# Two half projections of layer 1 moved into the last stage of layer 0

## The chip, the cores and the metric

The kernel runs on one core of a Trainium2 chip. The metric is the device time of one execution in microseconds; several runs are taken, and their median counts. Engines run side by side and meet only at semaphores: TensorE (PE) multiplies, VectorE (DVE), ScalarE (ACT) and GpSimd (POOL) work elementwise, SyncE (SP) issues most of the DMAs.

## The reference

A trunk of two layers on 1024 tokens of width 1024, all in float32. Each layer is `x = x + rmsnorm(mix(rmsnorm(x)))` and then `x = x + rmsnorm(ffn(rmsnorm(x)))`. Layer 0 (even) mixes with two kinds of attention, layer 1 (odd) with a sliding window of 128 tokens, 16 query heads, 2 key/value heads and a learned sink for each head. What matters here is the seam between them:

```python
h = rmsnorm(x, g[0])                       # layer 1, x is layer 0's result
q, k, v = split_cols(h @ w_qkv, ODD_SIZES) # 1024 x 1024 by 1024 x 1280
q, k = partial_rope(q, cos, sin), partial_rope(k, cos, sin)
```

and before it layer 0's down projection, `(gelu(gate) * val) @ w_out`, with 2816 rows in `w_out`.

## The kernel before, in words

**Products in three passes.** Each float32 factor is held as a hi part (rounded to fp32r) and a lo part (the rest), and each product is hi*hi + hi*lo + lo*hi. `three_passes` (L121) issues that for one weight block of 128 x 128 and one or two halves of 512 columns; every matmul in it loads its weights. A weight tile of 128 columns has 8 blocks (KT = 8), so a tile over both token halves is 8 x 3 x 2 = 48 matmuls, over one half 24. The hi part of a weight tile is an ACT copy of the loaded tile (L1968 in the trunk, L862 in the odd front), the lo part a subtraction on GpSimd (L2055, L985) or on VectorE (L2238).

**The trunk stage.** `trunk_stage` (L1722) is run once for each layer. It does the output projection of the mixer, the two norms around it, the 44 up tiles (NT_UP) with convolution and gate, and 66 down tiles (NT_DOWN = 3 x 22). The down projection goes in three passes over the 22 tiles of `w_out`, for token blocks 0 to 3, then 4 and 5, then 6 and 7 (BLOCKS). A down tile of the last pass is 2 blocks x 2 halves x 3 = 12 matmuls into ps[2] and ps[3]. The weights go round a ring of three hi/lo slots (`down_slot`, L1828) and four raw buffers (`raw_down`).

**The end of layer 0.** When a block's down product is complete, the block is normalised: ScalarE squares and sums it (`first`, L1930), VectorE scales it and adds x (`mix`, L2178, `add`, L2195), ScalarE stores it and squares it again (`second`, L1942), VectorE makes h, the normalised input of layer 1 (`scale`, L2197, the operation at L2206). TensorE turns h with 8 transposes (`turn`, L2064), and ScalarE and VectorE split what was turned into `act.hi` and `act.lo` (L1955, L2213). For blocks 0 to 5 that lies between later down tiles. Blocks 6 and 7, the last two, are turned behind all down tiles (L2171), into ps[0] and ps[1]. GpSimd has nothing to do in the down tiles.

**Between the stages** all engines meet at the end of the block, the semaphores of the stage are cleared (`recycle`, L103) and there is a barrier.

**The start of layer 1.** `OddFront` (L701) is the part of layer 1's trunk stage up to the output of the mixer. It projects h with 10 weight tiles: the keys (N_KEY = 0), the values (N_V = 1), eight of queries (from N_Q = 2). `project(n)` (L1038) writes prod[n % 2], which is ps[0] or ps[1], hi weights first (L375) and the lo pass behind them (L381). `take(n)` (L864, L872) copies it out. The order on the engines is written out by hand:

- TensorE: project(0), project(1) with rot(KEY) (L1027) behind its third block, project(2) with `turn_values(0)` (L1030, L1035) behind its third block, project(3) with turn_values(1) and rot, and so on. rot needs take(0); turn_values needs take(1).
- ScalarE: hi(0), hi(1), take(0), hi(2), pack_keys (L878, needs the rope of the keys), take(1), hi(3), take(2), hi(4), ...
- VectorE: rope(KEY) (L1158, L1159, L1162), the keys' lo parts (L1169), the copies of the turned values, then the ropes of the queries.
- SyncE loads tile n when the lo part of tile n - 2 is made (L828).

act.hi[0] and act.lo[0] hold token half 0, which is blocks 0 to 3; act.hi[1] and act.lo[1] hold blocks 4 to 7.

Of the kernel before, what the change touches and what calls it, by code (L numbers as in the profile page):

```python
# [6 lines left out]
F32 = mybir.dt.float32  # L7
# [8 lines left out]
P = 128  # L16
T = 1024
# [60 lines left out]
class Stage:  # L78
# [4 lines left out]
    def __init__(self, nc, name):  # L83
        self.nc, self.name, self.ctx = nc, name, ExitStack()
# [616 lines left out]
class OddFront:  # L701
# [5 lines left out]
    NG = 4 * TB  # L707
    LAST_SLOT = 4 * TB + 4

    def __init__(self, nc, g, st, base, act, new_act, w, sinks, w_mix, mix_rows, x_src, x_mid, gains, ps, stats, x_in, x_out, gain_in,  # L710
                 sq1, iv1, sq2, iv2, mixed, summed, h_ready):
        self.nc, self.g, self.act, self.new_act = nc, g, act, new_act
        self.w, self.sinks, self.w_mix, self.mix_rows = w, sinks, w_mix, mix_rows
# [10 lines left out]
        self.mraw = [at(f"mraw{k}", [P, D], F32, K + 32 * KB + 4 * KB * k) for k in range(KT)]  # L724
        self.mlo = [at(f"mlo{k}", [P, D], F32R, K + 32 * KB + 4 * KB * k) for k in range(KT)]
        W = K + 64 * KB
        self.raw = [at(f"raw{i}", [P, KT, P], F32, W + 4 * KB * i) for i in range(2)]
        self.w_hi = [at(f"w_hi{i}", [P, KT, P], F32R, W + 4 * KB * (2 + i)) for i in range(2)]
        self.w_lo = [at(f"w_lo{i}", [P, KT, P], F32R, W + 4 * KB * (4 + i)) for i in range(2)]
        self.prob = [at(f"prob{i}", [P, self.PAIRS, P], F32, W + 2 * KB * i) for i in range(2)]  # L730
        self.pT = [at(f"probT{i}", [P, self.PAIRS, P], F32, W + 2 * KB * (2 + i)) for i in range(2)]
        self.o = at("o", [P, 2, 2 * self.PAIRS, HD], F32, W + 8 * KB)
# [94 lines left out]

    def sync(self, sp, load_up):  # L828
        wv = self.w.rearrange("(k p) c -> p k c", p=P)
        for n in range(self.N_ALL):  # L830
            if n >= 2:
                sp.wait_ge(self.lo_done, n - 1)
            sp.dma_start(self.raw[n % 2][:], wv[:, :, self.COLUMN[n]:self.COLUMN[n] + P]).then_inc(self.w_in[n % 2], 16)
            if n == 1:
                sp.dma_start(self.sink[:].rearrange("p i s -> p (i s)"), self.sinks.partition_broadcast(P)).then_inc(self.sink_in, 16)
        sp.wait_ge(self.prod_done, self.N_ALL)
        for k in range(KT):
            for i, r in enumerate(self.mix_rows(k)):
                sp.dma_start(self.mraw[k][HD * i:HD * i + HD, :], self.w_mix[r:r + HD, :]).then_inc(self.m_in[k], 16)
        sp.wait_ge(self.q_lo, 32)  # L840
        sp.dma_start(self.g1[:], self.gains[0].partition_broadcast(P)).then_inc(self.gain_in, 16)
        sp.dma_start(self.g2[:], self.gains[1].partition_broadcast(P)).then_inc(self.gain_in, 16)
        rows = self.x_src.rearrange("(b p) d -> b p d", p=P)
        for b in range(TB):
            if b == 0:
                sp.wait_ge(self.rope_done, len(self.ROPED))
            else:
                sp.wait_ge(self.x_out[(b - 1) % 2], 16 * ((b - 1) // 2 + 1))
                sp.wait_ge(self.h_ready, b)
            sp.dma_start(self.x[:], rows[b]).then_inc(self.x_in[b % 2], 16)  # L850
            if b == TB - 2:
                load_up(0)
                load_up(1)

    def scalar(self, sc, split_w):
        N_KEY, N_V, N_Q, N_ALL, NG = self.N_KEY, self.N_V, self.N_Q, self.N_ALL, self.NG

        def hi(n):
            sc.wait_ge(self.w_in[n % 2], 16 * (n // 2 + 1))
            if n >= 2:  # L860
                sc.wait_ge(self.prod_done, n - 1)
            sc.activation(self.w_hi[n % 2][:], self.raw[n % 2][:], ACT.Copy).then_inc(self.hi_done, 1)  # L862

        def take(n):  # L864
            sc.wait_ge(self.prod_done, n + 1)
# [21 lines left out]
        def exp(n):  # L887
            nk = self.keys_of(self.where(n)[1])
            sc.wait_ge(self.nb_ready, n + 1)
            if n == 0:  # L890
                sc.wait_ge(self.lo_done, N_ALL)
# [86 lines left out]
    def gpsimd(self, pool, up_lo):  # L978
        pool.memset(self.v_even[:, :, :, HD:VW], 1.0).then_inc(self.ones_set, 1)
        pool.memset(self.v_odd[:, :, :, HD:VW], 1.0).then_inc(self.ones_set, 1)  # L980
        for n in range(self.N_ALL):
            pool.wait_ge(self.hi_done, n + 1)
            if n >= 2:
                pool.wait_ge(self.prod_done, n - 1)
            pool.tensor_tensor(self.w_lo[n % 2][:], self.raw[n % 2][:], self.w_hi[n % 2][:].bitcast(F32), ALU.subtract).then_inc(self.lo_done, 1)  # L985
        for k in range(KT):
            pool.wait_ge(self.m_hi, k + 1)
            pool.tensor_tensor(self.mlo[k][:], self.mraw[k][:], self.mhi[k][:].bitcast(F32), ALU.subtract).then_inc(self.m_lo, 1)
        for b in range(TB):
# [24 lines left out]
    def tensor(self, pe):  # L1014
# [21 lines left out]
            mm.then_inc(self.v_turned, 1)  # L1036

        def project(n):  # L1038
            pe.wait_ge(self.hi_done, n + 1)
            if n >= 2:  # L1040
                pe.wait_ge(self.taken, n - 1)
            outs = [self.prod[n % 2][:, h] for h in H]
            for k in range(KT):
                hi_weight_passes(pe, outs, self.w_hi[n % 2][:, k, :], [x[:, k, :] for x in act.hi], [x[:, k, :] for x in act.lo], k == 0)
                if k == 2 and n == N_KEY + 1:
                    rot(N_KEY)
                if k == 2 and n == N_Q:
                    turn_values(0)
                if k == 2 and n == N_Q + 1:
                    turn_values(1)  # L1050
                if k == 2 and n > N_Q + 1:
                    rot(n - 1)
                if k == 5 and n == N_Q + 1:
                    rot(N_Q)
            pe.wait_ge(self.lo_done, n + 1)
            for k in range(KT):
                mm = lo_weight_pass(pe, outs, self.w_lo[n % 2][:, k, :], [x[:, k, :] for x in act.hi], k == KT - 1)
            mm.then_inc(self.prod_done, 1)

        def scores(n):  # L1060
# [658 lines left out]
    return act  # L1719


def trunk_stage(nc, g, name, layer, act, w_mix, mix_rows, w_in, w_out, gains, x_src, x_mid, x_dst, onward, odd_mixer=None):  # L1722

# [79 lines left out]

    with Stage(nc, name) as st:
        st.sb("arena", [P, (194 * KB + 512 if odd_mixer else 129 * KB) // 4])
        ps = [st.ps(f"ps{i}", [P, T]) for i in range(4)]
# [14 lines left out]
        odd = odd_mixer and OddFront(nc, g, st, base, odd_input, act, *odd_mixer, w_mix, mix_rows, x_src, x_mid, gains, ps,  # L1823
                                     ([ss1, ss2], [std1, std2], [inv1, inv2]), x_in, x_out, gain_in[0],
                                     sq1, iv1, sq2, iv2, mixed, summed, h_ready)

        pass_of = lambda d: d // FT
        down_slot = lambda d: (NT_UP + d) % 3  # L1828
# [19 lines left out]
        with nc.Block() as block:  # L1848
            @block.sync
            def _(sp):  # L1850
# [59 lines left out]
                for d in range(NT_DOWN):  # L1910
# [13 lines left out]
                    if d == 2 * FT + 8:  # L1924
                        load_x(TB + 6)
                        load_x(TB + 7)

            @block.scalar
            def _(sc):
# [108 lines left out]
                for e in range(4, FT):  # L2038
                    prepare(2 * FT + e)
                    if e in (7, 8):  # L2040
                        split_h(TB + e - 3, ps[e - 7])
                first(TB + 6, ps[2])
                first(TB + 7, ps[3])
                second(TB + 6)
                second(TB + 7)
                split_h(TB + 6, ps[0])
                split_h(TB + 7, ps[1])
                for i in range(2):
                    sc.wait_ge(x_out[i], 16 * TB)

# [1 line left out]
            def _(pool):  # L2052
# [5 lines left out]
                    odd.gpsimd(pool, lo)  # L2058
                for u in range(2 if odd else 0, NT_UP):
                    lo(u)  # L2060

            @block.tensor
            def _(pe):
# [95 lines left out]
                for d in range(NT_DOWN):  # L2159
# [6 lines left out]
                    if d in (2 * FT + 4, 2 * FT + 5):  # L2166
# [1 line left out]
                        if onward:  # L2168
                            pe.wait_ge(mixed, TB + n + 1)
                        turn(TB + n, ps[n - 4])  # L2170
                for n in range(6, TB):  # L2171
                    if onward:
                        pe.wait_ge(lo_done, TB + n - 1)
                    turn(TB + n, ps[n - 6])

            @block.vector
            def _(dve):
# [126 lines left out]
                for n in range(TB + 6, TB + 8):  # L2304
                    scale(n)
                for n in range(TB + 6, TB + 8):
                    split_h(n, ps[n - TB - 6])


def build(nc, x, positions, norm_gains, even_w_in, even_b_forget, even_w_out, odd_w_qkv, odd_sinks, odd_w_out,  # L2310
# [5 lines left out]
    with Stage(nc, "main") as st:  # L2316
# [55 lines left out]
        with Stage(nc, "rest") as rs:  # L2372
# [6 lines left out]
            trunk_stage(nc, g, "l0", 0, act, even_w_out[0], lambda k: [P * k], ffn_w_in, ffn_w_out, (row(0, 1), row(0, 2), row(0, 3), row(1, 0)),  # L2379
                        x[0], x_mid, x_odd, True)  # L2380
            Stage.recycle(nc)
        trunk_stage(nc, g, "l1", 1, act, odd_w_out[0], lambda k: [HD * (4 * (k // 2) + k % 2), HD * (4 * (k // 2) + 2 + k % 2)], ffn_w_in, ffn_w_out, (row(1, 1), row(1, 2), row(1, 3), None),
                        x_odd, x_mid, out[0], False, (odd_w_qkv[0], odd_sinks))


_INS = ['x', 'positions', 'norm_gains', 'even_w_in', 'even_b_forget', 'even_w_out', 'odd_w_qkv', 'odd_sinks',
# [14 lines left out]
```

## Time and profile before

| | |
|---|---|
| median of 3 runs | 2650.26 us (2639.95 to 2651.22) |
| the profiled execution | 2648.2 us |
| its span | 2646.4 us |
| TensorE busy | 2476.6 us |
| mean granted clock of TensorE | 0.97 |
| end of the last down tile of layer 0 | 1545.6 us |
| first DMA issue of layer 1's stage | 1559.91 us |
| first matmul of layer 1 | 1564.88 us |

The profile is of one execution. Times in its rows are microseconds from the span's start; the granted clock is in parts of TensorE's full speed, 1.00 for 2.4 GHz. Matmuls overlap each other: what counts is the distance from start to start. In the timeline "x8" means eight instructions in a run, and the time in brackets is the idle time of the engine before them, with what ended it.

### The profile page before, as it was taken

The numbers are of one execution on the slowest core, as the hardware profiler recorded it, in microseconds if no ns is written. First come the engines' busy times: TensorE is split into PE (matmuls) and PEld (weight loads), VectorE is DVE, ScalarE is ACT, GpSimd is POOL, SyncE is SP. The second block draws the span as 40 slices with busy tenths as digits, with TensorE's granted clock in tenths as the row PEclk, the third lists the DMA queues.
The fourth block names the chain that finished last, engine by engine and source line by source line (L and its number), as shares of the span: only waits on it lengthen the run. The fifth ranks groups of instructions, "written<-read, shape, count | busy, mean of one in ns | idle before, by whom it ended". The sixth has DMA issues, their size and how long they took to land. (4 is left out here: it accounts for less than half of the span.)

```text
span 2646.4 us, 30903 instructions
## 1 busy us (share of the span) xinstructions
PE 2476.6 (94%) x12099; PEld 2069.7 (78%) x12099; DVE 1257.4 (48%) x2034; ACT 1079.6 (41%) x1615; POOL 417.9 (16%) x358
## 2 busy tenths in 40 slices
PE   6889879989799999999999979899799999999998
PEld 4668658889687888888887867698688888888877
DVE  4564667855443333333436634566433333334365
ACT  4445777766433222222325533455322222223344
POOL 2102103311001222222000011042322222210000
PEclk9999989999899999999999989899999999999999
DMA  4101000000331111111335721301211111114375
GB/s 143 33 16 48 25 17 25 25 1 1 112 110 49 48 50 52 50 48 48 112 99 182 236 88 40 88 25 50 87 48 48 48 48 48 48 40 135 96 246 175
DMA packets 164139, 191.27 MB, mean 72 GB/s; under 512 B 12020, under 2 KB 133204, under 8 KB 163996
## 3 DMA queue, kind: packets, MB, share of 16 engines
q1 hardware_dynamic: 158432, 171.79, 21.1%
q10 hardware_dynamic: 5564, 17.52, 1.7%
q8 instruction: 97, 1.59, 0.2%
q14 instruction: 46, 0.38, 0.0%
HBM read 172.41 MB, written 16.88 MB: 72 GB/s over the span
## 5 line engine op out<-in xcount | busy, mean ns | idle before, releaser
L2055 POOL TENSOR_TENSOR l_wlo<-l_raw,l_whi 128x1024 fp32r<-128x1024 f32 x88 | 212.3, 2412 | 854.9 <-ACT l_whi L1968 854.9
L126 PE MATMUL l_ps<-odd_act_hi,l_whi 128*128 128x512 f32 x704 | 221.5, 392 | 1.4 <-DVE odd_act_lo L1215 1.4
L126 PE MATMUL l_ps<-rest_hi,l_whi 128*128 128x512 f32 x704 | 219.5, 389 | 2.4 <-DVE rest_lo L2213 2.4
L126 PE MATMUL l_ps<-odd_act_lo,l_whi 128*128 128x512 f32 x704 | 221.1, 392 | 0.0
L126 PE MATMUL l_ps<-odd_act_hi,l_wlo 128*128 128x512 f32 x704 | 220.9, 391 | 0.0
L126 PE MATMUL l_ps<-rest_hi,l_wlo 128*128 128x512 f32 x704 | 219.4, 389 | 0.0
L126 PE MATMUL l_ps<-rest_lo,l_whi 128*128 128x512 f32 x704 | 219.3, 389 | 0.0
L2219 DVE SCALAR_TENSOR_TENSOR l_y_v<-l_ps,main_conv,l_y_v 128x1023 f32<-128x1023 f32 x44 | 56.4, 1283 | 337.7 <-ACT l_y_v L2008 337.7
L1968 ACT ACTIVATE l_whi<-l_raw 128x1024 fp32r<-128x1024 f32 x156 | 164.1, 1052 | 127.4 <-PE l_ps L126 120.3
L2008 ACT ACTIVATE l_y_g<-l_ps,main_conv 128x1024 f32<-128x1024 f32 x44 | 53.1, 1207 | 383.1 <-PE l_ps L126 383.1
L2219 DVE SCALAR_TENSOR_TENSOR l_y_g<-l_ps,main_conv,l_y_g 128x1023 f32<-128x1023 f32 x44 | 56.4, 1283 | 284.2 <-ACT l_y_g L2008 284.2
L126 PEld LDWEIGHTS l_ps<-odd_act_hi,l_whi 128*128 128x128 f32 x704 | 133.3, 189 | 29.6 <-DVE odd_act_lo L1215 1.8
L126 PEld LDWEIGHTS l_ps<-rest_hi,l_whi 128*128 128x128 f32 x704 | 132.1, 188 | 30.0 <-DVE rest_lo L2213 2.6
L126 PEld LDWEIGHTS l_ps<-odd_act_hi,l_wlo 128*128 128x128 f32 x704 | 133.3, 189 | 27.9
L126 PEld LDWEIGHTS l_ps<-odd_act_lo,l_whi 128*128 128x128 f32 x704 | 133.3, 189 | 27.6
L126 PEld LDWEIGHTS l_ps<-rest_hi,l_wlo 128*128 128x128 f32 x704 | 132.1, 188 | 27.5
L126 PEld LDWEIGHTS l_ps<-rest_lo,l_whi 128*128 128x128 f32 x704 | 132.1, 188 | 27.3
L2008 ACT ACTIVATE l_y_v<-l_ps,main_conv 128x1024 f32<-128x1024 f32 x44 | 53.1, 1206 | 238.8 <-PE l_ps L126 238.8
L2238 DVE TENSOR_TENSOR l_wlo<-l_raw,l_whi 128x1024 fp32r<-128x1024 f32 x68 | 83.2, 1223 | 108.8 <-ACT l_whi L1968 108.8
L126 PE MATMUL l_ps<-l_whi,l_ghie 128*128 128x512 f32 x376 | 116.3, 390 | 4.0 <-issue 3.1
L126 PE MATMUL l_ps<-l_wlo,l_ghie 128*128 128x512 f32 x376 | 115.9, 389 | 0.0
L126 PE MATMUL l_ps<-l_whi,l_gloe 128*128 128x512 f32 x376 | 115.7, 389 | 0.0
(355 smaller groups left out, 5303.8 us busy)
## 6 DMA issues: line engine op xcount, KB each, us to landing
l_raw<-in_ffn_w_in SPq DMA_DIRECT2D x88, 512.0 KB, 3.8
l_raw<-in_ffn_w_out SPq DMA_DIRECT2D x68, 512.0 KB, 3.7
l_rawl<-in_ffn_w_out SPq DMA_DIRECT2D x44, 512.0 KB, 3.8
wring_raw<-in_even_w_in SPq DMA_DIRECT2D x20, 512.0 KB, 3.8
l_rawe<-in_ffn_w_out SPq DMA_DIRECT2D x20, 512.0 KB, 3.6
odd_raw<-in_odd_w_qkv SPq DMA_DIRECT2D x10, 512.0 KB, 3.9
setup_xin<-in_x SPq DMA_DIRECT2D x8, 512.0 KB, 5.8
fox_negc<-negc_dram SPq DMA_DIRECT2D x8, 512.0 KB, 3.9
```

The costliest lines, as they stand in the source:

```text
L126: mm = pe.matmul(o, w, m, start=a, stop=z)
L1968: sc.activation(whi[s % 3][:], src[:], ACT.Copy).then_inc(whi_done, 1)
L2008: sc.activation(y[x][:], ps[u % 4][:], ACT.Identity, bias=biasw(x, i), scale=tapw(x, 2, i)).then_inc(tap2[x], 1)
L2055: pool.tensor_tensor(wlo[u % 3][:], raw_up[u % 2][:], whi[u % 3][:].bitcast(F32), ALU.subtract).then_inc(up_lo, 1)
L2219: dve.scalar_tensor_tensor(out=y[x][:, 1:T], in0=src[:, 0:T - 1], scalar=tapw(x, 1, i), in1=y[x][:, 1:T], op0=ALU.mult, op1=ALU.add).then_ ...
L2238: dve.tensor_tensor(wlo[slot][:], raw_down(d)[:], whi[slot][:].bitcast(F32), ALU.subtract).then_inc(down_lo, 1)
```

## The change

Layer 0's trunk stage is told what comes next (`ahead`: the odd weights and their column order). Behind its last loads SyncE loads weight tiles 0 and 1 of layer 1 into two raw buffers. Behind its last prepare ScalarE makes their hi parts in the two ring slots that down tiles 63 and 64 leave, and GpSimd the lo parts. Behind the last down tile TensorE projects token half 0 with both tiles, 24 matmuls each, into ps[0] and ps[1], and turns blocks 6 and 7 behind the third and the fifth block of the second tile, into ps[2] and ps[3]. In layer 1 project(0) and project(1) then do only token half 1, without a load or a split; SyncE, ScalarE and GpSimd begin with tile 2. The PSUM tiles are allocated once for both layers, the ring of the odd weights starts with the two slots, and so hi(n) waits for project(n - 2) for every n.

```diff
--- before.py
+++ after.py
@@ class OddFront
+    EARLY = 2
...
-        self.raw = [at(f"raw{i}", [P, KT, P], F32, W + 4 * KB * i) for i in range(2)]
-        self.w_hi = [at(f"w_hi{i}", [P, KT, P], F32R, W + 4 * KB * (2 + i)) for i in range(2)]
-        self.w_lo = [at(f"w_lo{i}", [P, KT, P], F32R, W + 4 * KB * (4 + i)) for i in range(2)]
+        self.raw = [at(f"raw{i}", [P, KT, P], F32, W + 4 * KB * (2 + i)) for i in range(2)]
+        ring = [at(f"w_hi{i}", [P, KT, P], F32R, W + 16 * KB * (1 - i)) for i in range(2)]
+        self.w_hi = early[0] + [ring[n % 2] for n in range(self.EARLY, self.N_ALL)]
+        ring = [at(f"w_lo{i}", [P, KT, P], F32R, W + 16 * KB * (1 - i) + 4 * KB) for i in range(2)]
+        self.w_lo = early[1] + [ring[n % 2] for n in range(self.EARLY, self.N_ALL)]
@@ OddFront.sync
-        for n in range(self.N_ALL):
-            if n >= 2:
-                sp.wait_ge(self.lo_done, n - 1)
+        for n in range(self.EARLY, self.N_ALL):
+            if n >= self.EARLY + 2:
+                sp.wait_ge(self.lo_done, n - 1 - self.EARLY)
             sp.dma_start(self.raw[n % 2][:], wv[:, :, self.COLUMN[n]:self.COLUMN[n] + P]).then_inc(self.w_in[n % 2], 16)
-            if n == 1:
+            if n == self.EARLY + 1:
@@ OddFront.scalar
         def hi(n):
-            sc.wait_ge(self.w_in[n % 2], 16 * (n // 2 + 1))
-            if n >= 2:
-                sc.wait_ge(self.prod_done, n - 1)
-            sc.activation(self.w_hi[n % 2][:], self.raw[n % 2][:], ACT.Copy).then_inc(self.hi_done, 1)
+            sc.wait_ge(self.w_in[n % 2], 16 * ((n - self.EARLY) // 2 + 1))
+            sc.wait_ge(self.prod_done, n - 1)
+            sc.activation(self.w_hi[n][:], self.raw[n % 2][:], ACT.Copy).then_inc(self.hi_done, 1)
...
-        hi(0)
-        hi(1)
+        hi(2)
         take(N_KEY)
-        hi(2)
         pack_keys()
@@ OddFront.gpsimd
-        for n in range(self.N_ALL):
-            pool.wait_ge(self.hi_done, n + 1)
-            if n >= 2:
-                pool.wait_ge(self.prod_done, n - 1)
-            pool.tensor_tensor(self.w_lo[n % 2][:], self.raw[n % 2][:], self.w_hi[n % 2][:].bitcast(F32), ALU.subtract).then_inc(self.lo_done, 1)
+        for n in range(self.EARLY, self.N_ALL):
+            pool.wait_ge(self.hi_done, n + 1 - self.EARLY)
+            pool.tensor_tensor(self.w_lo[n][:], self.raw[n % 2][:], self.w_hi[n][:].bitcast(F32), ALU.subtract).then_inc(self.lo_done, 1)
@@ OddFront.tensor
         def project(n):
-            pe.wait_ge(self.hi_done, n + 1)
-            if n >= 2:
+            left = slice(1, 2)
+            if n >= self.EARLY:
+                pe.wait_ge(self.hi_done, n + 1 - self.EARLY)
                 pe.wait_ge(self.taken, n - 1)
-            outs = [self.prod[n % 2][:, h] for h in H]
+                left = slice(0, 2)
+            outs, x_hi, x_lo = [self.prod[n % 2][:, h] for h in H][left], act.hi[left], act.lo[left]
...
-            pe.wait_ge(self.lo_done, n + 1)
+            if n >= self.EARLY:
+                pe.wait_ge(self.lo_done, n + 1 - self.EARLY)
@@ trunk_stage
+        if ahead:
+            next_in, next_hi, next_lo = [st.sem(f"next_in{i}") for i in range(2)], st.sem("next_hi"), st.sem("next_lo")
+            free_from = [NT_DOWN - 3 + i for i in range(2)]
+            next_raw, next_w = raw_far["l"], [[part[(NT_UP + d) % 3] for d in free_from] for part in (whi, wlo)]
@@ trunk_stage, SyncE, behind the loop over load_down
+                for i in range(2 if ahead else 0):
+                    w, columns = ahead
+                    wait_down_lo(sp, NT_DOWN - 4 + i)
+                    sp.dma_start(next_raw[i][:], w.rearrange("(k p) c -> p k c", p=P)[:, :, columns[i]:columns[i] + P]).then_inc(next_in[i], 16)
@@ trunk_stage, ScalarE, behind the last prepare
+                for i in range(2 if ahead else 0):
+                    sc.wait_ge(next_in[i], 16)
+                    wait_down_tile(sc, free_from[i])
+                    sc.activation(next_w[0][i][:], next_raw[i][:], ACT.Copy).then_inc(next_hi, 1)
                 first(TB + 6, ps[2])
                 first(TB + 7, ps[3])
                 second(TB + 6)
                 second(TB + 7)
-                split_h(TB + 6, ps[0])
-                split_h(TB + 7, ps[1])
+                split_h(TB + 6, ps[2])
+                split_h(TB + 7, ps[3])
@@ trunk_stage, GpSimd
+                for i in range(2 if ahead else 0):
+                    pool.wait_ge(next_hi, i + 1)
+                    pool.tensor_tensor(next_w[1][i][:], next_raw[i][:], next_w[0][i][:].bitcast(F32), ALU.subtract).then_inc(next_lo, 1)
@@ trunk_stage, TensorE, behind the down tiles
-                for n in range(6, TB):
-                    if onward:
-                        pe.wait_ge(lo_done, TB + n - 1)
-                    turn(TB + n, ps[n - 6])
+                for i in range(2 if ahead else 0):
+                    pe.wait_ge(next_lo, i + 1)
+                    if i == 0:
+                        pe.wait_ge(lo_done, TB + 6)
+                    for k in range(KT):
+                        three_passes(pe, [ps[i][:, H[0]]], next_w[0][i][:, k, :], next_w[1][i][:, k, :], [act.hi[0][:, k, :]], [act.lo[0][:, k, :]],
+                                     k == 0, k == KT - 1)
+                        if i and k in (2, 4):
+                            turn(TB + 5 + k // 2, ps[1 + k // 2])
+                for n in range(TB if ahead else 6, TB):
+                    turn(TB + n, ps[n - 4])
@@ trunk_stage, VectorE, and build
-                    split_h(n, ps[n - TB - 6])
+                    split_h(n, ps[n - TB - 4])
...
+            trunk_ps = Stage(nc, "trunk")
+            ps = [trunk_ps.ps(f"ps{i}", [P, T]) for i in range(4)]
```

## Rows read from the trace of the kernel before

**Rows 1.** The page: TensorE's busy time, and the chain that ended last by line.
```profile
PE 2476.6 (94%) x12099; PEld 2069.7 (78%) x12099; DVE 1257.4 (48%) x2034; ACT 1079.6 (41%) x1615; POOL 417.9 (16%) x358
...
PE l_ps L126 28%; PE l_ps L375 3%; PE l_ps L381 1%; PE l_ps L1099 1%; PE l_ps L1085 1%; PE l_ps L1074 1%; PE l_ps L1073 1%; PE l_ps L1027 1%; DMA l_rawl<-in_ffn_w_out 0%; DVE l_wlo L2238 0%; PE l_ps L1149 0%; DVE odd_h L1231 0%; PE l_ps L1144 0%; DVE main_cos L1221 0%; DVE odd_q L145 0%
```

**Rows 2.** Windows of 2 us, TensorE only: length, busy (count), granted clock, DMA share, GB/s.
```profile
820.00:822.00 2.00, 0.00 (x0) 1.00 0.00 0
1548.00:1550.00 2.00, 0.00 (x0) 0.60 0.31 129
1566.00:1568.00 2.00, 2.00 (x6) 0.50 0.03 8
1568.00:1570.00 2.00, 2.00 (x8) 0.78 0.71 182
```

**Rows 3.** Timeline of layer 0's tail: start, duration, engine, line, operation, [idle before it].
```profile
1533.23 1.23 DVE L2238 TENSOR_TENSOR l_wlo<-l_rawl,l_whi 128x1024 fp32r<-128x1024 f32 x1 [1.16 <-ACT l_whi L1968]
...
1537.58 1.06 ACT L1968 ACTIVATE l_whi<-l_raw 128x1024 fp32r<-128x1024 f32 x1 [1.35 <-PE l_ps L126]
...
1544.32 1.02 ACT L1932 ACTIVATE l_junkl<-l_ps 128x1024 bf16<-128x1024 f32 x1 [5.38 <-PE l_ps L126]
...
1545.03 0.61 PE L126 MATMUL l_ps<-l_whi,l_glol 128*128 128x512 f32 x2
...
1547.31 1.23 DVE L2195 TENSOR_TENSOR l_x0l<-l_x0l,l_h0l 128x1024 f32<-128x1024 f32 x1
...
1551.30 1.28 DVE L2206 SCALAR_TENSOR_TENSOR l_h0l<-l_x0l,l_inv,l_g2l 128x1024 f32<-128x1024 f32 x1
...
1552.73 1.94 PE L2069 MATMUL l_ps<-main_const,l_h0l 128*128 128x128 f32 x8 [7.09 <-DVE l_h0l L2206]
...
1553.30 1.28 DVE L2206 SCALAR_TENSOR_TENSOR l_h1l<-l_x1l,l_inv,l_g2l 128x1024 f32<-128x1024 f32 x1
...
1557.77 1.22 DVE L2213 TENSOR_TENSOR rest_lo<-l_ps,rest_hi 128x1024 fp32r<-128x1024 f32 x1 [0.78 <-ACT rest_hi L1955]
```

**Rows 4.** The chain of waits across the start of layer 1: start, duration, what.
```profile
1559.91 3.83 DMA odd_raw<-in_odd_w_qkv
...
1564.88 9.40 PE l_ps L375 x32
1574.27 3.63 PE l_ps L381 x16
...
1580.63 1.72 PE l_ps L1027 x4
...
1593.23 0.87 PE l_ps L1035 x8
1594.11 4.57 PE l_ps L375 x20
```

**Rows 5.** Timeline of TensorE in layer 0: half-token matmuls and the last turn before a split.
```profile
808.67 0.39 PE L126 MATMUL l_ps<-rest_hi,l_whi 128*128 128x512 f32 x1
...
818.64 0.39 PE L126 MATMUL l_ps<-rest_hi,l_wlo 128*128 128x512 f32 x1
818.87 1.03 PE L2069 MATMUL l_ps<-main_const,l_h1m 128*128 128x128 f32 x8
822.28 0.50 PE L126 MATMUL l_ps<-rest_hi,l_whi 128*128 128x512 f32 x1 [2.37 <-DVE rest_lo L2213]
```

**Rows 6.** Timeline of ScalarE behind project(0) of layer 1.
```profile
1577.94 1.03 ACT L872 ACTIVATE odd_fm<-l_ps 128x1024 f32<-128x1024 f32 x1 [11.56 <-PE l_ps L381]
1578.86 1.05 ACT L862 ACTIVATE odd_w_hi<-odd_raw 128x1024 fp32r<-128x1024 f32 x1
1586.12 4.31 ACT L878 ACTIVATE odd_k_hi<-odd_fm 64x1024 fp32r<-64x1024 f32 x4 [6.21 <-DVE odd_fm L1162]
```

**Rows 7.** The keys' lo copies on VectorE (min/median/max), and GpSimd's timeline there.
```profile
L1169 DVE TENSOR_TENSOR odd_k_lo<-odd_fm,odd_k_hi x4: 1216/1220/3292, 1590.5 to 1596.3; 64x1024 fp32r<-64x1024 f32 x4
...
1592.74 2.43 POOL L985 TENSOR_TENSOR odd_w_lo<-odd_raw,odd_w_hi 128x1024 fp32r<-128x1024 f32 x1 [10.40 <-ACT odd_w_hi L862]
```

More of the change, by code:

```diff
@@ L708, with __init__ @@
     LAST_SLOT = 4 * TB + 4
-    def __init__(self, nc, g, st, base, act, new_act, w, sinks, w_mix, mix_rows, x_src, x_mid, gains, ps, stats, x_in, x_out, gain_in,
+    EARLY = 2
+    def __init__(self, nc, g, st, base, act, new_act, w, sinks, early, w_mix, mix_rows, x_src, x_mid, gains, ps, stats, x_in, x_out, gain_in,
                  sq1, iv1, sq2, iv2, mixed, summed, h_ready):
@@ L890, in exp @@
             if n == 0:
-                sc.wait_ge(self.lo_done, N_ALL)
+                sc.wait_ge(self.lo_done, N_ALL - self.EARLY)
             if n >= 2:
@@ L1038, in project @@
         def project(n):
-            pe.wait_ge(self.hi_done, n + 1)
-            if n >= 2:
+            left = slice(1, 2)
+            if n >= self.EARLY:
+                pe.wait_ge(self.hi_done, n + 1 - self.EARLY)
                 pe.wait_ge(self.taken, n - 1)
-            outs = [self.prod[n % 2][:, h] for h in H]
+                left = slice(0, 2)
+            outs, x_hi, x_lo = [self.prod[n % 2][:, h] for h in H][left], act.hi[left], act.lo[left]
             for k in range(KT):
-                hi_weight_passes(pe, outs, self.w_hi[n % 2][:, k, :], [x[:, k, :] for x in act.hi], [x[:, k, :] for x in act.lo], k == 0)
+                hi_weight_passes(pe, outs, self.w_hi[n][:, k, :], [x[:, k, :] for x in x_hi], [x[:, k, :] for x in x_lo], k == 0)
                 if k == 2 and n == N_KEY + 1:
@@ L1054, in project @@
                     rot(N_Q)
-            pe.wait_ge(self.lo_done, n + 1)
+            if n >= self.EARLY:
+                pe.wait_ge(self.lo_done, n + 1 - self.EARLY)
             for k in range(KT):
-                mm = lo_weight_pass(pe, outs, self.w_lo[n % 2][:, k, :], [x[:, k, :] for x in act.hi], k == KT - 1)
+                mm = lo_weight_pass(pe, outs, self.w_lo[n][:, k, :], [x[:, k, :] for x in x_hi], k == KT - 1)
             mm.then_inc(self.prod_done, 1)
@@ L1719, in act_halves, with trunk_stage @@
     return act
-def trunk_stage(nc, g, name, layer, act, w_mix, mix_rows, w_in, w_out, gains, x_src, x_mid, x_dst, onward, odd_mixer=None):
+def trunk_stage(nc, g, name, layer, act, w_mix, mix_rows, w_in, w_out, gains, x_src, x_mid, x_dst, onward, ps, odd_mixer=None, ahead=None):
     NT_UP, BLOCKS = 2 * FT, ((0, 1, 2, 3), (4, 5), (6, 7))
@@ L1807, in trunk_stage @@
         st.sb("arena", [P, (194 * KB + 512 if odd_mixer else 129 * KB) // 4])
-        ps = [st.ps(f"ps{i}", [P, T]) for i in range(4)]
         raw_in = [st.sem(f"raw_in{i}") for i in range(4)]
@@ L2306, in _ @@
                 for n in range(TB + 6, TB + 8):
-                    split_h(n, ps[n - TB - 6])
+                    split_h(n, ps[n - TB - 4])
+    return next_w if ahead else None
 def build(nc, x, positions, norm_gains, even_w_in, even_b_forget, even_w_out, odd_w_qkv, odd_sinks, odd_w_out,
@@ L2378, in build @@
             Stage.recycle(nc)
-            trunk_stage(nc, g, "l0", 0, act, even_w_out[0], lambda k: [P * k], ffn_w_in, ffn_w_out, (row(0, 1), row(0, 2), row(0, 3), row(1, 0)),
-                        x[0], x_mid, x_odd, True)
+            trunk_ps = Stage(nc, "trunk")
+            ps = [trunk_ps.ps(f"ps{i}", [P, T]) for i in range(4)]
+            early = trunk_stage(nc, g, "l0", 0, act, even_w_out[0], lambda k: [P * k], ffn_w_in, ffn_w_out, (row(0, 1), row(0, 2), row(0, 3), row(1, 0)),
+                        x[0], x_mid, x_odd, True, ps, ahead=(odd_w_qkv[0], OddFront.COLUMN))
             Stage.recycle(nc)
         trunk_stage(nc, g, "l1", 1, act, odd_w_out[0], lambda k: [HD * (4 * (k // 2) + k % 2), HD * (4 * (k // 2) + 2 + k % 2)], ffn_w_in, ffn_w_out, (row(1, 1), row(1, 2), row(1, 3), None),
-                        x_odd, x_mid, out[0], False, (odd_w_qkv[0], odd_sinks))
+                        x_odd, x_mid, out[0], False, ps, odd_mixer=(odd_w_qkv[0], odd_sinks, early))
+        trunk_ps.__exit__(None, None, None)
 _INS = ['x', 'positions', 'norm_gains', 'even_w_in', 'even_b_forget', 'even_w_out', 'odd_w_qkv', 'odd_sinks',
```

## The prediction

> **What bounds the kernel now.** The page first: TensorE is busy for 94% of the span, and the chain that ended last runs mostly over its matmuls, above all the projections [rows 1]. So a stretch is shortened by filling a hole of TensorE, or by removing work from it. The change removes none: it moves 48 matmuls into a hole. The question is how long the hole is, and what else sets its length.
>
> The windows of TensorE and the timeline of layer 0's last microseconds answer that. The last down tile's matmuls are over at 1545.6; TensorE then waits 7.09 us for the normalisation of block 6, turns blocks 6 and 7 (from 1552.73 on, 1.94 us for the first, and as much for the second), and waits again until 1564.88 [rows 3, 4]. In the first hole the granted clock falls (0.60 in the window 1548 to 1550); it is 0.50, which is 1.2 GHz, still at 1566 to 1568, and comes back in the window behind that [rows 2]. The second hole consists of a hi and a lo copy of block 7 (to 1557.77 + 1.22 = 1558.99), the end of the stage with its barriers (0.92 us, until SyncE issues at 1559.91), the weight load (3.83) and, in the 1.1 us left, the hi copy of the weights [rows 3, 4].
>
> The chain of waits then gives the price of the first three projections. Project(0) takes 9.40 us for 32 matmuls and 3.63 for 16. Project(2) ends at 1594.11 + 4.57 + 3.63 (its lo pass, 16 matmuls again) = 1602.31 [rows 4]. That is my anchor: from project(3) on, both kernels do the same work in the same order.
>
> **The change, part by part.** All positions are on the time axis of before.
>
> Loads. SyncE's last two waits are for VectorE's lo parts of down tiles 62 and 63; the second is over at 1533.23 + 1.23 = 1534.46 [rows 3]. Nothing is queued behind these loads. At 3.83 us [rows 4] the second lands at 1538.3.
>
> Hi copies. ScalarE does them after its last prepare (1537.58 and on), and waits for TensorE to finish tiles 63 and 64. A down tile is 12 matmuls of 0.227 us (20 matmuls in 4.57 [rows 4] give 0.228; the 44 starts from 808.67 to 818.64 [rows 5] give 0.2266), 2.72 us. The last ends at 1545.6, so tiles 63 and 64 end about 1540.2 and 1542.9. The copies run 1540.3 to 1541.3 and 1543.0 to 1544.1. Queued behind them is the Square of block 6, at 1544.32 [rows 3]: 0.2 us of slack, cost nothing. If TensorE's clearance came late, the normalisation would slip by the same amount.
>
> Lo copies. GpSimd needs 2.43 us each [rows 7]: 1541.4 to 1543.8 and 1544.1 to 1546.6. TensorE wants the first at 1545.5 and the second 5.4 us later. Cost nothing.
>
> Here one row speaks against the change. Of VectorE's four identical copies at L1169 three took 1.22 us and one 3.29 [rows 7], while GpSimd's lo copy was running (1592.74, 2.43 us): a collision costs up to 2.07 us. In the tail the first VectorE operation on two SBUF operands is the add at 1547.31 [rows 3], 0.7 us after the second lo copy is over, so I take nothing; the other end is 2.07 us, because the add is on the chain to the turns. The Trainium skill, SBUF — State Buffer, section "SBUF: two separate sides", says that VectorE with two SBUF inputs and GpSimd reading SBUF take a port pair in turn, each holding it for the whole instruction. By that rule the row is explained and the sum stands unless the second lo copy is late by over 0.7 us; then the stage would end later by what is left of that copy.
>
> TensorE's tail. It goes on at 1545.5, with the clock at 1.00. 24 matmuls of project(0)'s half and 9 of project(1)'s: 33 x 0.227 = 7.5, to 1553.0; block 6 is ready since 1551.30 + 1.28 = 1552.58 [rows 3], so no wait. A turn at full clock costs 0.87 us (the turn of values in the chain [rows 4]). Six matmuls, 1.36, then the turn of block 7 at 1555.2, ready since 1553.30 + 1.28 = 1554.58 [rows 3]. From such a turn's start to the end of its lo copy took 3.4 us (818.87 to 822.28 [rows 5]), so to 1558.6; TensorE's last nine matmuls end at 1558.2, beside it. The end of the stage at 0.92 us as before; four more semaphores are cleared, for which no row has a price; I bound it by 0 and by that 0.92 once more, and take 0, since the 0.92 clears several dozen. Layer 1 starts at 1559.5.
>
> Head of layer 1. Project(0)'s other half needs no load, no copy: 24 x 0.227 = 5.44 us. The loads and copies of tiles 2 and 3 go alongside. But hi(2) now waits for that half's end, not only for its load, and stands before take(0) on ScalarE. Hi, then take: 1.0 us to the start of the take, 1.03 for it [rows 6]. TensorE reaches rot after only 6 matmuls, 1.36 us, and waits 0.7. With rot's 1.72 [rows 4], rot ends 5.44 + 2.07 + 1.72 = 9.23 us into the stage.
>
> **A new wait.** Turn_values(0) needs take(1), which ScalarE does behind the packing of the keys, which waits for VectorE's rope. From rot's end (1582.35) to the packing's start (1586.12) it is 3.77 us, the packing is 4.31 [rows 4, 6], the take 1.03, with 0.05 of hand-over 9.2 us. Before, TensorE had 36 matmuls of project(1) and 12 of project(2) to do meanwhile. After, it has 18 and 12: 30 x 0.227 = 6.8. It stalls 2.4 us, on ScalarE's take. Then 0.87 + 4.57 + 3.63 = 9.07 to the end of project(2) [rows 4]. GpSimd's lo copy of tile 2 ends some 0.2 us before the rope starts, that of tile 3 hits the keys' lo copies as it does now, and nobody waits for these.
>
> **Sum.** 1559.5 + 9.23 + 9.2 + 9.07 = 1587.0 against 1602.3: **15.3 us gained**, 0.58%. As a check by terms: idle before is 7.1 + 8.2, after it is 1.3 + 0.7 + 2.4, so 10.9 less; half clock cost 2 x (1.94 - 0.87) = 2.1 in the turns and 13.03 - 10.9 = 2.1 in project(0); together 15.1. The profiled execution took 2648.2 (span 2646.4), which gives 2632.9. The median of the runs is 2650.3, which gives 2635.0; the three runs lie between 2640.0 and 2651.2. I take 2634. About 0.5%, 13.2 us, is what a measurement of this kernel can tell from no change, so the forecast lies only 2 us beyond.
>
> After project(3) nothing is anchored to absolute time: loads, rope and packing follow TensorE's progress, so I expect all of the gain to reach the end.
>
> **Rivals.**
>
> *The new stalls cost more than their length (within 0.5%, 0.35 with the spread of the runs).* TensorE now has idle stretches of 1.3, 0.7 and 2.4 us in some 20 us. For it: in the idle of 7.1 us the clock fell, and after the second hole it was back only in the window 1568 to 1570, when project(0) had run since 1564.88 [rows 2, 4]. Against it: in 820 to 822 TensorE sat idle too, with the clock at 1.00 [rows 2]. Once through the slow phase costs what project(0) shows, 2.1 us: gain 13.2, time 2635 to 2637. With a port collision of 2.07 on top, gain 11, time 2637 to 2639. The same class holds a stage start of TensorE that is later than SyncE's, by up to a microsecond.
>
> *The stalls are smaller (0.05).* If ScalarE's chain is done sooner, up to 3.1 us more: gain 18.4, 2630 to 2632. The dependencies speak against it.
>
> *Slower (0.03).* Place: projects 0 to 3 of layer 1. If the three idles bring the clock to half and the stalls keep it there, a matmul costs up to twice 0.227, 0.227 more. 67 such matmuls give all of the 15.3 back; the whole of projects 0 to 3 has 24 + 24 + 48 + 48 = 144 of them after the stage's start, loses 32.7 and ends at 2665. It decides from the 67th on, and from the 126th the kernel is over 13.2 us slower. Against it: unbroken work of 5.4 us stands at the very start. The Trainium skill, TensorE: Matmul & The Clock Gate, section "What's actually happening", says that activity releases the throttle and idleness sets it again; the rows agree.
>
> *The change doesn't do what it says.* If TensorE at 1545.5 had to wait for the first lo copy, the hole would stay in part. The turns stand behind the moved matmuls in its order, so such a wait pushes the whole tail back. The lo copy has 1.7 us of slack; at worst it is the second case, at 2635 to 2637.
>
> **How the numbers follow.** Forecast, with the gain between 13.3 and 17: 0.57. Less, or hidden in the spread of the runs: 0.35. More: 0.05. Slower: 0.03. Hence faster 0.62, same 0.35, slower 0.03. The range: from below by the lowest run less the gain, 2640 - 15.3 = 2624.7; from above by the median less a gain of 7 to 8 (the stalls once through the slow phase, a collision, and a slow stage start, with 2 of spread). I give 2624 to 2643.
>
> **What would show it.** Right: TensorE's line without a hole between 1545 and 1558; the clock at 1.00 in all windows from 1540 to 1600; half-token matmuls behind L126 from weights in layer 0's ring, followed by L375 on one half at the stage's start some 0.9 us after the last lo copy; a wait of about 0.7 us before rot and one of 2.4 us before the turn of values, both put down to ScalarE's L872; project(3) beginning 15.3 us earlier. Wrong: a clock of 0.50 after the stage's start; an add at L2195 of over 2 us in the tail; a longer barrier; or a gain of 15 at project(3) of which less is left at the end, where a later wait for something other than TensorE would have to have taken it.

## The result and the profile after

Eight runs of each kernel: the changed kernel has a median of 2632.28 us (2628.31 to 2638.46), the kernel before 2648.05 (2639.95 to 2651.22). The two medians differ by 15.8 us. The measured ratio, which is not simply that of the medians, is 0.9948, with a 95% interval from 0.9931 to 0.9966: 13.8 us, between 9 and 18. A second comparison on another occasion (e_take and r_after below) gave medians of 2632.84 against 2645.58, ratio 0.9953 (0.9941 to 0.9965). The profiled execution took 2636.05, with a span of 2634.3.

In this trace the tail of layer 0 comes 3.83 us later than in the trace of before (Square of block 6 at 1548.15 against 1544.32 [rows 3]); where that comes from is told with r_before. To compare, take 3.83 off every time in the following. The timeline of the tail, all engines, cut to what the prediction named:

```profile
1544.13 1.06 ACT L2055 ACTIVATE l_whi<-l_rawl 128x1024 fp32r<-128x1024 f32 x1 [1.35 <-PE trunk_ps L126]
1545.27 2.40 POOL L2077 TENSOR_TENSOR l_wlo<-l_rawl,l_whi 128x1024 fp32r<-128x1024 f32 x1 [279.01 <-ACT l_whi L2055]
...
1546.85 1.06 ACT L2055 ACTIVATE l_whi<-l_rawl 128x1024 fp32r<-128x1024 f32 x1 [1.66 <-PE trunk_ps L126]
1547.99 2.40 POOL L2077 TENSOR_TENSOR l_wlo<-l_rawl,l_whi 128x1024 fp32r<-128x1024 f32 x1 [0.32 <-ACT l_whi L2055]
1548.15 1.02 ACT L1942 ACTIVATE l_junkl<-trunk_ps 128x1024 bf16<-128x1024 f32 x1 [0.24 <-PE trunk_ps L126]
...
1551.15 1.23 DVE L2219 TENSOR_TENSOR l_x0l<-l_x0l,l_h0l 128x1024 f32<-128x1024 f32 x1
...
1556.80 1.03 PE L2086 MATMUL trunk_ps<-main_const,l_h0l 128*128 128x128 f32 x8
...
1559.05 1.03 PE L2086 MATMUL trunk_ps<-main_const,l_h1l 128*128 128x128 f32 x8
...
1561.18 1.22 DVE L2237 TENSOR_TENSOR rest_lo<-trunk_ps,rest_hi 128x1024 fp32r<-128x1024 f32 x1 [1.03 <-ACT rest_hi L1965]
```

The two hi copies (L2055) and the two lo copies (L2077) lie where they were put; 0.24 us of ScalarE's idle time is left in front of the Square. Blocks 6 and 7 are turned at 1556.80 and 1559.05, which is 1552.97 and 1555.22 on the old axis, behind 33 and 39 matmuls. TensorE has no hole until the stage ends.

The head of layer 1, TensorE's rows that carry a wait, and those around them:

```profile
1563.41 0.47 PE L375 MATMUL trunk_ps<-rest_hi,l_whi 128*128 128x512 f32 x1 [1.27 <-PEq L106]
...
1571.26 1.98 PE L1026 MATMUL trunk_ps<-odd_fm,main_const 128*128 128x512 f32 x4 [0.77 <-ACT odd_fm L875]
...
1582.41 1.97 PE L1034 MATMUL trunk_ps<-main_const,odd_fm 128*128 128x128 f32 x8 [2.33 <-ACT odd_fm L875]
1584.03 1.20 PE L375 MATMUL trunk_ps<-rest_hi,odd_w_hi 128*128 128x512 f32 x2
1585.03 1.00 PE L375 MATMUL trunk_ps<-rest_lo,odd_w_hi 128*128 128x512 f32 x2
1585.87 0.62 PE L375 MATMUL trunk_ps<-rest_hi,odd_w_hi 128*128 128x512 f32 x2
```

The clock in windows of TensorE (length, busy, granted clock, DMA share, GB/s):

```profile
1578.00:1580.00 2.00, 2.00 (x10) 1.00 0.00 0
1580.00:1582.00 2.00, 0.09 (x1) 1.00 0.00 0
1582.00:1584.00 2.00, 1.58 (x8) 0.61 0.00 0
1584.00:1586.00 2.00, 2.00 (x7) 0.54 0.00 0
1586.00:1588.00 2.00, 2.00 (x11) 1.00 0.31 70
```

The first row of that group is the last full one before the wait of 2.33 us. Behind the wait the clock is at 0.61 and 0.54: half speed for most of 4 us. The chain of waits over the same stretch shows what it cost:

```profile
1571.26 2.00 PE trunk_ps L1026 x4
...
1581.34 1.03 ACT odd_fm L875
...
1582.41 1.97 PE trunk_ps L1034 x8
1584.38 5.30 PE trunk_ps L375 x20
1589.68 3.63 PE trunk_ps L381 x16
```

Against [rows 4] the turn of values takes 1.97 instead of 0.87, and the 20 matmuls behind it 5.30 instead of 4.57.

**The measure D.** For the experiments I use the time from the start of ScalarE's Square of block 6 to the end of project(2). It is 57.98 us before (1602.30 - 1544.32) and 45.16 after (1593.31 - 1548.15): 12.8 us gained in the seam.

### The profile page after: what moved, and what is told of

Same layout as the page of the kernel before. It is cut to its first block and busy times, and to the rows that moved or that the text cites. A ratio compares the mean times of both kernels' runs of the same rounds, so it can differ in the third digit from the quotient of the medians.

```text
span 2634.3 us, 30896 instructions
## 1 busy us (share of the span) xinstructions
PE 2477.6 (94%) x12099; PEld 2071.3 (79%) x12099; DVE 1257.8 (48%) x2034; ACT 1079.3 (41%) x1615; POOL 418.1 (16%) x358
## 5 line engine op out<-in xcount | busy, mean ns | idle before, releaser
L126 PE MATMUL trunk_ps<-rest_hi,l_whi 128*128 128x512 f32 x720 | 226.5, 390 | 2.4 <-DVE rest_lo L2237 2.4
L126 PE MATMUL trunk_ps<-rest_lo,l_whi 128*128 128x512 f32 x720 | 226.2, 390 | 0.0
L126 PE MATMUL trunk_ps<-rest_hi,l_wlo 128*128 128x512 f32 x720 | 226.2, 390 | 0.0
L126 PE MATMUL trunk_ps<-odd_act_hi,l_whi 128*128 128x512 f32 x704 | 221.4, 392 | 1.4 <-DVE odd_act_lo L1217 1.4
L126 PE MATMUL trunk_ps<-odd_act_lo,l_whi 128*128 128x512 f32 x704 | 220.9, 391 | 0.0
L126 PE MATMUL trunk_ps<-odd_act_hi,l_wlo 128*128 128x512 f32 x704 | 220.9, 391 | 0.0
L126 PEld LDWEIGHTS trunk_ps<-rest_hi,l_whi 128*128 128x128 f32 x720 | 135.5, 188 | 30.8 <-DVE rest_lo L2237 2.6
L126 PEld LDWEIGHTS trunk_ps<-rest_hi,l_wlo 128*128 128x128 f32 x720 | 135.6, 188 | 28.3
L126 PEld LDWEIGHTS trunk_ps<-rest_lo,l_whi 128*128 128x128 f32 x720 | 135.5, 188 | 27.9
L126 PEld LDWEIGHTS trunk_ps<-odd_act_lo,l_whi 128*128 128x128 f32 x704 | 133.3, 189 | 27.6
```

The costliest lines, as they stand in the source:

```text
L126: mm = pe.matmul(o, w, m, start=a, stop=z)
```

## The experiments

Each edit stands against the changed kernel.

### e_take: ScalarE's order

```diff
-        hi(2)
         take(N_KEY)
+        hi(2)
+        take(N_V)
         pack_keys()
         for n in range(N_V, N_ALL):
-            take(n)
+            if n > N_V:
+                take(n)
```

> Edit: in the changed kernel ScalarE takes project(0) before hi(2), and takes project(1) before it packs the keys. Measure D: from the start of ScalarE's Square of block 6 in layer 0's tail to the end of project(2) of layer 1; 57.99 us before, 45.16 in the changed kernel's profile. Theory (the changed kernel's two new stalls, 0.77 before rot and 2.33 before the turn of values, come from ScalarE's order alone, and the slow matmuls behind the second, 1.8 us, come from the clock that fell there): both stalls gone, granted clock 1.00 from 1540 to 1600, D 40.2, 4.9 us less. Rival A (the wait only moves: the keys are packed later, and TensorE then waits for VectorE's copies of the values or keys): D 42 to 45. Rival B (the slow stretch is not the clock's but a contention at the turn of values): stalls gone, slow stretch stays, D 42.

Measured: D 39.97. No wait of TensorE from the stage's start (1.27 us, as in the changed kernel) to project(3), and the clock 1.00 throughout. The runs: 2627.6 us median (2626.1 to 2631.29, 6 runs) against 2645.58 (17 runs) of the kernel before, ratio 0.993 (0.9918 to 0.9941), where the changed kernel beside it has 0.9953 (0.9941 to 0.9965). The theory holds; 5.2 us come from the order of three instructions on ScalarE. This version beats both kernels.

### e_takev and e_swap: the two halves of that edit

e_takev keeps `hi(2)` ahead of `take(N_KEY)` and only moves `take(N_V)`; e_swap only puts `take(N_KEY)` ahead of `hi(2)`.

> Edit: in the changed kernel only the take of project(1) is moved ahead of the packing of the keys; hi(2) stays ahead of take(0). D is 45.16 in the changed kernel (two traces), 39.97 with both edits. Theory (the edits add up; the stall of 2.33 and the slow clock behind it belong to this one): the wait of 0.77 before rot stays, no wait before the turn of values, clock 1.00, D 40.8 to 41.0. Rival (the clock's fall is brought about by all idle time of the seam together, so it may fall even so): a window of 0.5 to 0.6 stays, D 42.5.

Measured: D 40.98, the wait of 0.77 stays, the clock stays at 1.00. As expected: 4.2 us for this half.

> Edit: in the changed kernel only take(0) is put ahead of hi(2). Theory (the wait before rot goes, everything behind it comes 0.8 us earlier, the wait of 2.33 and the fall of the clock stay as they are): D 44.3. Rival (the idle of 2.33 alone does not bring the clock down, as an idle of 2.37 at 820 didn't before; it took the idles of 1.27 and 0.77 ahead of it too): clock 1.00 behind the wait, D 42.5.

Measured: D 45.24. Nothing gained, against both expectations, and so the two halves don't simply add up: alone this one is worth nothing, on top of e_takev 1.0 us (40.98 to 39.97). The wait before rot is gone, but the one before the turn of values has grown. Timeline rows of e_swap, GpSimd, VectorE and TensorE:

```profile
1573.71 2.39 POOL L984 TENSOR_TENSOR odd_w_lo<-odd_raw,odd_w_hi 128x1024 fp32r<-128x1024 f32 x1 [7.69 <-ACT odd_w_hi L865]
...
1574.77 2.42 DVE L1160 TENSOR_TENSOR odd_fm<-odd_fm,main_cos 128x1024 f32<-128x1024 f32 x1 [9.87 <-PE trunk_ps L1026]
...
1585.09 1.97 PE L1034 MATMUL trunk_ps<-main_const,odd_fm 128*128 128x128 f32 x8 [3.51 <-ACT odd_fm L875]
```

With rot earlier by 0.8 us, VectorE's product with the cosines, which reads two SBUF operands, now begins while GpSimd makes the lo part of tile 2 (1573.71 + 2.39 = 1576.10). It takes 2.42 us; in the changed kernel, where that copy ran from 1570.37 to 1572.71, it began behind it and took 1.23:

```profile
1570.37 2.34 POOL L984 TENSOR_TENSOR odd_w_lo<-odd_raw,odd_w_hi 128x1024 fp32r<-128x1024 f32 x1 [6.84 <-ACT odd_w_hi L865]
...
1573.28 1.23 DVE L1160 TENSOR_TENSOR odd_fm<-odd_fm,main_cos 128x1024 f32<-128x1024 f32 x1 [10.87 <-PE trunk_ps L1026]
```

The rope's product thus ends at the same distance from the Square as before the edit (26.55 us, 26.36 in the changed kernel), and all that waits for the rope comes no earlier. So the wait of 0.77 had been keeping the two engines apart. They hinder each other here with no semaphore between them. In e_take the same stretch to 2.42 is there, but the take of project(1) no longer stands behind the rope. The Trainium skill's rule on the shared port pair (SBUF — State Buffer, "SBUF: two separate sides") says that such a VectorE operation, once GpSimd's instruction has started first, waits for its end. The trace agrees: waiting from 1574.77 to GpSimd's end at 1576.10 and then 1.23 for itself would be 2.56 us, and it measured 2.42.

### e_port: the collision by design

```diff
                 for i in range(2 if ahead else 0):
                     pool.wait_ge(next_hi, i + 1)
+                    if i:
+                        pool.wait_ge(mixed, TB + 7)
```

> Edit: in the changed kernel GpSimd's second early lo copy waits until VectorE has scaled block 6, so that it begins with VectorE's add of two SBUF operands and runs beside the next ones; TensorE needs its result only 5.4 us after the last down tile. Theory (such a pair takes turns, as one of the keys' lo copies showed with 3.29 us instead of 1.22): the add of block 6 or of block 7 or GpSimd's copy is stretched by 1 to 2 us, and D grows by as much, to 46 to 47.2. Rival (they run side by side here): all at 1.22 and 2.4, D 45.2.

Measured: D 45.60, 0.44 more. The timeline of e_port in the tail:

```profile
1546.37 1.23 DVE L2221 TENSOR_TENSOR l_x0l<-l_x0l,l_h0l 128x1024 f32<-128x1024 f32 x1
...
1546.48 3.37 POOL L2079 TENSOR_TENSOR l_wlo<-l_rawl,l_whi 128x1024 fp32r<-128x1024 f32 x1 [3.59 <-DVE l_h0l L2214]
...
1549.02 1.92 DVE L2221 TENSOR_TENSOR l_x1l<-l_x1l,l_h1l 128x1024 f32<-128x1024 f32 x1
```

The add of block 6 starts before GpSimd and keeps its 1.23; GpSimd's copy, which would be 2.40, is stretched to 3.37, as if it had begun when the add was over at 1547.60; and the add of block 7 is stretched to 1.92, as if it had waited for that copy's end at 1549.85. The mechanism is as the theory has it, and its price on the path less than a half of what I gave it, since only 0.7 us were added to the add, and layer 1 starts 0.44 later (15.70 behind the Square instead of 15.26).

### e_split: load and split early, no early matmuls

TensorE's loop of `three_passes` in layer 0's tail is left out, and `left` is `slice(0, 2)` for all tiles.

> Edit: the changed kernel with the two tiles loaded and split in layer 0, but without the early matmuls: blocks 6 and 7 are turned alone, and project(0) and project(1) do both halves in layer 1. It parts the gain into the cover of load and split, and the filling of the normalisation hole. Theory: TensorE waits 7.1 us in the tail as before, turns at half clock, begins project(0) about 1.0 us after the last lo copy instead of 5.9, still at half clock; D 53.0 (5.0 less than before, 7.8 more than the changed kernel). Rival (load and split were the main thing, the matmuls add little): D below 50. Rival (the matmuls alone matter): D 57 to 58.

Measured: D 53.96, 4.0 us less than before. TensorE waits 7.00 us in the tail, and 3.32 between the last turn and project(0), which starts at half clock and takes from 1561.16 to 1575.09, 13.9 us (before: 13.0). Ten runs: 2640.85 against 2645.58, ratio 0.9984 (0.9975 to 0.9993). The wait in front of project(0) is 4.9 us shorter than before (8.20), as the theory had it. The 1.0 us that D lies above the theory is project(0) itself, which goes at half clock for longer. So of the 12.8 us about 4 belong to the cover of load and split, and 8.8 to the matmuls in the hole with the clock that they keep up, less what the two new waits of layer 1 cost. That is the split in this order of the two edits. The other order is not to be had, since the early matmuls need the split weights.

### e_last: the turns behind the early matmuls

```diff
-                        if i and k in (2, 4):
-                            turn(TB + 5 + k // 2, ps[1 + k // 2])
-                for n in range(TB if ahead else 6, TB):
+                for n in range(6, TB):
                     turn(TB + n, ps[n - 4])
```

> Edit: the changed kernel with the turns of blocks 6 and 7 behind all 48 early matmuls, not among them. Theory (the lo copy of block 7 closes the stage, and TensorE's own work is as long as the normalisation chain by luck): the stage ends 2.1 us later, D 47.3, and up to 2 more if the clock falls in the then longer idle at the seam. Rival (the place of the turns doesn't matter, the normalisation or a DMA closes the stage): D 45.2.

Measured: D 49.05, 3.9 us more. TensorE's rows:

```profile
1558.13 1.03 PE L2086 MATMUL trunk_ps<-main_const,l_h0l 128*128 128x128 f32 x8
1559.00 1.04 PE L2086 MATMUL trunk_ps<-main_const,l_h1l 128*128 128x128 f32 x8
1563.62 0.58 PE L375 MATMUL trunk_ps<-rest_hi,l_whi 128*128 128x512 f32 x1 [3.58 <-PEq L106]
```

The stage's first matmul comes at 1563.62, 17.53 us behind the Square instead of 15.26: 2.3 us for the place of the turns. The rest, 1.6 us, is the clock: the idle time at the seam has grown to 3.58 us, and in project(0) the clock is 0.50 from 1564 to 1566 and 0.69 from 1566 to 1568.

### e_turn4: more work ahead of the wait

```diff
-                if k == 2 and n == N_Q:
+                if k == 4 and n == N_Q:
                     turn_values(0)
```

> Edit: in the changed kernel the turn of values stands behind the fifth block of project(2), not behind the third, so TensorE has 8 more matmuls (1.8 us) to do before it needs ScalarE's take. Theory (what follows the wait at half clock follows from its length): the wait falls from 2.33 to 0.5, the clock stays at 1.00, D falls by 1.8 for the wait and by 1.8 for the clock, from 45.16 to 41.5. Rival (the clock falls there for another reason, such as the turn's own low load or the many small idles): the wait falls to 0.5, the clock falls all the same, D 43.3.

Measured: D 41.75; the wait is 0.52, the clock 1.00 in every window, and the turn takes 1.09 in the timeline where the changed kernel has 1.97. As expected: 3.4 us for moving one turn by two blocks. The single time is 2626.71, beside 2643.26 for the kernel before.

### r_after and r_before: how much is the execution

> The changed kernel once more, for a second trace and its times beside the one before on the same chip. Theory: the seam is fixed in length, D 45.2 within 0.3, save for the clock, whose fall behind the stall of 2.33 us may or may not come again (43.3 if it doesn't). The rest of the difference between the two medians (15.8 shown, 12.8 in the seam) is a spread between executions that lies outside the seam, in stages that are the same in both kernels. Rival: the change acts outside the seam too, so that the attention stages of layer 0 (start of fox to start of the turn stage 295.3 us before, 297.1 in the changed kernel) differ from before by the same amount in each trace.

> The kernel before once more, for a second trace. Theory: D is fixed by the program, 58.0 within 0.3, and the stages outside the seam differ from the first trace by a few microseconds where they did between traces of the changed kernel (the fox stage 160.4 or 163.6 us, the last down pass 124.4 to 128.9). Rival: the fox stage and the last pass have one length in the kernel before and another in the changed one.

Measured: r_after has D 45.16 again, with waits of 1.27, 0.77 and 2.34 and the fallen clock. r_before has 57.70, 0.28 less, since its clock came back sooner in project(0) (8.98 us for the 32 matmuls instead of 9.40 [rows 4]) while its weight load took 0.14 more (3.97). The stages outside the seam, from the starts of their operations in each trace (us; "fox stage" is from the first scores of one of layer 0's two attentions to the first of the other, "first gelu tile" from the last turn of block 6 in the mixer's norms to ScalarE's first read of an up tile, "down passes 2 and 3" from the end of layer 1's first down pass to that of its third, each taken at VectorE's scaling of the first block behind it):

| trace | fox stage | first gelu tile | seam, Square to first scores | down passes 2 and 3 | span |
|---|---|---|---|---|---|
| before | 160.4 | 20.2 | 146.9 | 128.9 | 2646.4 |
| r_before | 160.4 | 21.7 | 146.6 | 125.6 | 2641.4 |
| after | 163.6 | 21.8 | 134.1 | 126.1 | 2634.3 |
| r_after | 160.4 | 21.8 | 134.1 | 124.4 | 2629.3 |
| e_take | 163.6 | 21.8 | 128.9 | 125.0 | 2629.5 |
| e_takev | 160.4 | 20.2 | 129.9 | 128.3 | 2626.8 |
| e_swap | 165.2 | 21.8 | 134.2 | 124.7 | 2635.5 |
| e_port | 160.4 | 20.2 | 134.5 | 125.0 | 2628.9 |
| e_split | 163.6 | 20.2 | 142.9 | 125.1 | 2639.1 |
| e_last | 163.6 | 20.2 | 138.0 | 124.6 | 2634.7 |
| e_turn4 | 160.3 | 21.7 | 130.7 | 124.3 | 2624.9 |

The seam goes by the program. The fox stage, the first gelu tile and the down passes go by the execution: the fox stage is 160.4, 163.6 or 165.2 in kernels that are the same there, and so on. The 3.83 us by which the tail of layer 0 came later in the trace of after are made up of 3.2 in the fox stage and 1.6 in the first gelu tile, less 1.0 in all else ahead of it. The first gelu tile is the plainest. In both traces of before TensorE is idle for 2.37 us there; in the first [rows 2] the clock stays at 1.00, in r_before it falls:

```profile
816.00:818.00 2.00, 1.37 (x11) 1.00 0.00 0
818.00:820.00 2.00, 0.26 (x1) 0.88 0.00 0
820.00:822.00 2.00, 2.00 (x5) 0.50 0.00 0
822.00:824.00 2.00, 2.00 (x8) 0.76 0.00 0
```

Two traces of before and nine of its descendants can't exclude that the change acts a little outside the seam, but nothing in the table asks for it. It does mean that 5 us between two medians of few runs may come from elsewhere: the kernel before alone had medians of 2650.26, 2648.05 and 2645.58 us, and its two traces differ by 5.0 us in span. The gain of the change is best read from D, 12.5 to 12.8 us, which is 0.48%; both measured ratios hold it (0.9948 and 0.9953).

## Why the prediction was right, and where it was off

The time (2634.0 against 2632.3), the side and the range were right. The mechanism was right but for one thing, the clock behind the new wait. By the seam alone, the gain of 12.8 us lies just below the 13.3 to 17 of the forecast's main case and in the case "less", to which it gave 0.35. Of its own signs, "the clock at 1.00 in all windows from 1540 to 1600" and "project(3) beginning 15.3 us earlier" did not come true, and its first sign of being wrong, a clock of 0.50 after the stage's start, did (0.61 and 0.54 over two windows of 2 us). By its steps:

- *Loads, hi and lo copies.* Right, to 0.1 us: the idle time of 0.24 in front of the Square, nothing slipped. The collision in the tail did not take place, for the reason given.
- *TensorE's tail.* Right, once the 3.83 is taken off: turns at 1552.97 and 1555.22 for 1553.0 and 1555.2, the first matmul of layer 1 at 15.26 us behind the Square for 15.2. Clearing four more semaphores can't be seen: the first matmul comes 1.01 us after the last lo copy, where 0.92 was the distance to SyncE's issue before.
- *The wait before rot.* 0.77 for 0.7. But project(0)'s half took 5.74 us instead of 5.44 (3.91 + 1.83 in the chain of waits), and rot and its hand-over 2.00 instead of 1.72. In e_swap, where rot doesn't wait, it took 1.75.
- *The wait before the turn of values.* 2.33 for 2.4, put down to ScalarE's take (L872 before, L875 now), as forecast.
- *What failed* is the term behind it: "Then 0.87 + 4.57 + 3.63 = 9.07 to the end of project(2)", at full clock. It measured 1.97 + 5.30 + 3.63 = 10.90, 1.83 more. The sum said 15.3 gained, the seam gave 12.8: 1.8 of the 2.5 missing are this, 0.3 is rot, and 0.3 is project(0)'s half. That was priced under the first rival (once through the slow phase, 2.1 us, gain 13.2), and this rival took place. I had held against it the idle stretch in 820 to 822 with its clock at 1.00 [rows 2]. That was one execution's luck: r_before shows the same idle time with a clock of 0.50. Of the eleven traces in the table five have the fast value of the first gelu tile (20.2) and six the slow one (21.7 or 21.8), and the clock behind that idle time is 1.00 in the five and 0.50 to 0.61 in the six (the 2 us behind the wait).
- *e_turn4, e_takev and e_take* show that the wait itself is the cause: with 0.52 or none at that place the clock stays up in all three; with 2.33 or 2.34, or 3.51, it fell in all five traces (after, r_after, e_last, e_port, e_swap).
- *The gain reaches the end.* Right: in the table the seam's column keeps the order and the difference of D, and behind it nothing is given back: from the first scores to the end of layer 1's first down pass it is 817.3 to 818.7 us in all eleven traces, and the 128.9 and 125.6 of the down passes belong to one kernel.
- *The measured median* moved by 15.8 us in the first comparison and 12.7 in the second. That the first came out at the 15.3 of my sum is chance; my sum was right by its terms to the extent told above, and no further.
- *GpSimd's and VectorE's collision in the head* ("ends some 0.2 us before the rope starts") was seen, and its margin was 0.57 us in the trace (1572.71 to 1573.28). I used it for nothing; e_swap shows that it decides what the wait before rot is worth.

What stays open: what in an execution decides whether an idle time of 2.4 us brings the clock down. At the seam it did in all traces with it; at 820 in six of eleven.

## What to carry to other kernels

When a unit of work is taken out of a sequence to fill a hole elsewhere, look at what that unit had been covering: here half of two projections had hidden a chain of rope, packing and take, and 5 of the 18 us that the move can give were lost to it until ScalarE's takes were put ahead of the hi copy and of the packing (e_take, 18.0 us in the seam instead of 12.8). Price a new idle stretch of TensorE like the 2.33 us here with the fall of the clock behind it, about 1.8 us (behind the waits of 0.52, 0.77 and 1.27 us it stayed at 1.00), and don't take one trace in which the clock held for a rule. And before removing a small wait, see what it holds apart: GpSimd's and VectorE's reads of SBUF took turns as soon as it was gone.

## What was not expected of the hardware

- The same idle time of TensorE, 2.37 us at the same place of the same program, left the granted clock at 1.00 in one execution and brought it to 0.50 in another. And the clock need not fall while TensorE idles: in e_port it goes on again at 1578.07 with the clock still at 1.00 until 1578.4, and only then, at work, falls to half. In e_last the whole idle time of 3.58 us is at 1.00 and the fall comes 0.2 us behind it.
- That GpSimd and VectorE take turns was on record with the prediction, but not that it would meet the rope: VectorE's product of two SBUF operands took 2.42 us instead of 1.23 beside GpSimd's subtraction, whose own duration stayed at 2.39 when it had started first; when VectorE had started first (e_port), GpSimd's was stretched to 3.37 and VectorE's next one to 1.92.
